# Two-block transformer kernel: product order behind three norms, place of the splits, a wait for GpSimd's masks

## The reference

```python
def rms_norm_2(x, gain):
    xf = x.astype(jnp.float32)
    y = xf * lax.rsqrt(jnp.mean(xf * xf, axis=-1, keepdims=True) + NORM_EPS)
    return (y * gain.astype(jnp.float32)).astype(x.dtype)

def swiglu_2(h, w_gate, w_up, w_down):
    return (jax.nn.silu(h @ w_gate) * (h @ w_up)) @ w_down
```

## Time and profile before

| | |
|---|---|
| executions shown | 1966.95, 1968.44, 1965.23 us; median 1966.95 |
| the profiled execution | 1967.34 us; span of its instructions 1965.5 us |
| mean granted clock of TensorE | 0.975 of full |
| PE busy | 1848.6 us, 94% of the span, 15010 matmuls |
| DVE busy | 1156.8 us, 59% |
| ACT busy | 770.1 us, 39% |
| POOL busy | 300.6 us, 15% |
| DMA | 266 MB, mean 135 GB/s |
| chain that ended last | PE 75%, DVE 12%, POOL 5%, ACT 5%, rest 3% |

### The profile page before, as it was taken

How to read it: one execution, slowest core, us unless ns; L and a number is a source line. 1 busy time by engine, 2 the same in 40 slices (tenths; PEclk the granted TensorE clock), 3 DMA queues, 4 the chain that set the end, 5 groups by cost and what they waited for, 6 DMA issues and landing times.

```text
span 1965.5 us, 34448 instructions
## 1 busy us (share of the span) xinstructions
PE 1848.6 (94%) x15010; PEld 1629.9 (83%) x15010; DVE 1156.8 (59%) x1715; ACT 770.1 (39%) x1073; POOL 300.6 (15%) x264
## 2 busy tenths in 40 slices
PE   7999888999999978987999999999998999999998
PEld 5777556878888868856999999989988778899997
DVE  4643575554353337666655486555767778576654
ACT  4432563221122224455443443343455444344332
POOL 0011001899180010100000100002001111000000
PEclk9998998999999988999999999999999999999999
DMA  8344212565353222203555655544431111245551
GB/s 347 107 156 177 75 44 86 175 212 189 135 182 125 87 76 70 81 22 108 174 191 174 214 182 179 186 150 158 153 119 45 45 45 67 88 172 177 188 187 71
DMA packets 40759, 266.24 MB, mean 135 GB/s; under 512 B 4512, under 2 KB 4640, under 8 KB 13344
## 3 DMA queue, kind: packets, MB, share of 16 engines
q1 hardware_dynamic: 35712, 244.10, 35.5%
q0 software_dynamic: 4608, 16.78, 2.7%
q10 hardware_dynamic: 288, 3.15, 0.4%
HBM read 262.96 MB, written 1.05 MB: 134 GB/s over the span
## 4 chain that ended last, share of the span: by engine, by line
PE 75%; DVE 12%; POOL 5%; ACT 5%; issue 2%; DMA 2%; DVEq 0%; ACTq 0%; POOLq 0%
PE ps L641 18%; PE ps L643 18%; PE ps L642 18%; DVE W L621 2%; POOL work L1101 2%; PE ps L1641 2%; POOL work L1102 1%; PE ps L1003 1%; PE ps L647 1%; PE ps L1428 1%; PE ps L648 1%; PE ps L649 1%; PE ps L2372 1%; ACT W L612 1%; PE ps L2390 1%
## 5 line engine op out<-in xcount | busy, mean ns | idle before, releaser
L621 DVE TENSOR_TENSOR W<-ring,W 128x2048 fp32r<-128x2048 f32 (+2 forms) x194 | 439.5, 2267 | 247.2 <-ACT W L612 246.8
L612 ACT ACTIVATE W<-ring 128x2048 fp32r<-128x2048 f32 (+2 forms) x194 | 359.2, 1854 | 123.9 <-PE ps L643 114.0
L641 PE MATMUL ps<-h_lat,W 128*128 128x256 f32 x1056 | 301.4, 285 | 6.1 <-DVE h_lat L807 4.2
L643 PE MATMUL ps<-h_lat,W 128*128 128x256 f32 x1056 | 299.4, 283 | 0.0
L642 PE MATMUL ps<-h_lat,W 128*128 128x256 f32 x1056 | 299.4, 283 | 0.0
L641 PEld LDWEIGHTS ps<-h_lat,W 128*128 128x128 f32 x1056 | 203.2, 192 | 8.2 <-issue 4.6
L642 PEld LDWEIGHTS ps<-h_lat,W 128*128 128x128 f32 x1056 | 203.3, 193 | 0.3 <-issue 0.2
L643 PEld LDWEIGHTS ps<-h_lat,W 128*128 128x128 f32 x1056 | 203.3, 192 | 0.0
L748 POOL TENSOR_TENSOR work<-work 128x256 f32<-128x256 f32 (+1 forms) x42 | 41.1, 977 | 955.7 <-ACT work L730 768.5
L984 DVE TENSOR_TENSOR work<-work,ps 128x256 f32<-128x256 f32 (+1 forms) x88 | 43.0, 488 | 189.2 <-ACT work L959 189.1
L641 PE MATMUL ps<-hidden_lat,W 128*128 128x256 f32 x528 | 149.4, 283 | 0.0
(11 more groups left out here) (405 smaller groups left out, 4308.6 us busy)
## 6 DMA issues: line engine op xcount, KB each, us to landing
ring<-w_up_dram SPq DMA_DIRECT2D x88, 1024.0 KB, 4.9
ring<-w_down_dram SPq DMA_DIRECT2D x43, 1024.0 KB, 4.9
ring<-w_ada_dram SPq DMA_DIRECT2D x32, 1024.0 KB, 6.5
work<-w_ada_dram POOLq DMA_DIRECT2D x32, 512.0 KB, 4.1
ring<-w_rkv_dram SPq DMA_DIRECT2D x13, 1024.0 KB, 4.9
ring<-w_fm_dram SPq DMA_DIRECT2D x10, 1024.0 KB, 5.0
ring<-w_out_dram SPq DMA_DIRECT2D x8, 1024.0 KB, 4.9
ring<-w_gates_dram SPq DMA_DIRECT2D x16, 512.0 KB, 3.6
```

What stands on the lines that cost most here:

```text
L612: act.activation(slots[SLOT[s]][:, 0, 0:cols], ring[:, u % RING, 0:cols], ACT.Copy).then_inc(w_high, 1)
L621: dve.tensor_tensor(slots[SLOT[s]][:, 1, 0:cols], ring[:, u % RING, 0:cols], slots[SLOT[s]][:, 0, 0:cols], ALU.subtract).then_inc(w_low, 1)
L641: pe.matmul(o, slots[SLOT[s]][:, 0, at:at + cols], high, start=first, stop=False)
L643: return pe.matmul(o, slots[SLOT[s]][:, 1, at:at + cols], high, start=False, stop=final)
```

## The change

Four edits.

1. In `dve_residual` and `act_residual`, where a norm follows, the split of the last step (m = 7) is no longer made ahead of that step, but behind all 8 steps, with the same argument.
2. In `act_high` for norm 0, ACT makes the split of the second unit of tma0 behind the first tile's high parts; ahead of it stays the first unit's.
3. Behind norms 1, 3 and 6 PE takes each arriving tile for two results. At norm 1 these are the gate and the up half of the first unit (two banks of PSUM), at norm 3 the gate halves of the first two units of up1, at norm 6 the first feature tiles of the first two units of qk. The other halves follow. The number of matmuls stays.
4. In `pool_rwkv` GpSimd waits, ahead of the second of its five masks, for `rw_T0`, DVE's end of L2713.

```diff
@@ dve_residual
             for m in range(KT):
-                dve_split(dve, s0 + ((m + 1) * kt - 1) // TPU + 1 + AHEAD)
+                if m < KT - 1 or norm is None:
+                    dve_split(dve, s0 + ((m + 1) * kt - 1) // TPU + 1 + AHEAD)
...
             if norm in LATE:
                 dve_late_low(dve, norm, KT - 1)
+            if norm is not None:
+                dve_split(dve, s0 + (KT * kt - 1) // TPU + 1 + AHEAD)
@@ act_residual
             for m in range(KT):
-                act_split(act, s0 + ((m + 1) * kt - 1) // TPU + 1 + AHEAD)
+                if m < KT - 1 or norm is None:
+                    act_split(act, s0 + ((m + 1) * kt - 1) // TPU + 1 + AHEAD)
...
+            if norm is not None:
+                act_split(act, s0 + (KT * kt - 1) // TPU + 1 + AHEAD)
@@ act_high
                     ins.then_inc(h_high, 1)
+                if r == 0 and m == 0:
+                    act_split(act, FIRST_OF_KIND["tma0"] + 2)
@@ pe_ffn
                 for i in range(f):
                     s, g = FIRST_OF_KIND[up] + i, FIRST_GROUP[up] + i
-                    bank = pe_group(pe, g)
+                    bank = GROUPS[g][0] if r == 1 and i == 1 else pe_group(pe, g)
                     pe_weights(pe, s)
+                    if r == 0 and x == 0 and i == 0:
+                        for k in range(KT):
+                            pe_h_tile(pe, norm, k)
+                            for half in range(2):
+                                mm = weight_tile(pe, ps[:, bank + half, 0:n], s, (half * KT + k) * P, P, h[:, k, 0, :], h[:, k, 1, :],
+                                                 k == 0, k == KT - 1)
+                        mm.then_inc(group_done, 1)
+                        continue
+                    if r == 1 and i == 0:
+                        pe_weights(pe, s + 1)
+                        second = pe_group(pe, g + 1)
+                        for k in range(KT):
+                            pe_h_tile(pe, norm, k)
+                            for y, b in ((0, bank), (1, second)):
+                                weight_tile(pe, ps[:, b, 0:n], s + y, k * P, P, h[:, k, 0, :], h[:, k, 1, :], k == 0, k == KT - 1)
                     for half in range(2):
+                        if r == 1 and i < 2 and half == 0:
+                            continue
@@ pe_qkv (two_tiles loses its arguments norm and late)
+            for i in range(2):
+                banks.append(pe_group(pe, g0 + i))
+                pe_weights(pe, s0 + i)
+            for k in range(KT):
+                pe_h_tile(pe, 6, k)
+                for i in range(2):
+                    weight_tile(pe, ps[:, banks[i], 0:T], s0 + i, k * P, P, h_mix[:, k, 0, :], h_mix[:, k, 1, :], k == 0, k == KT - 1)
+            for i in range(2):
+                for k in range(KT):
+                    mm = weight_tile(pe, ps[:, banks[i], T:2 * T], s0 + i, (KT + k) * P, P, h_mix[:, k, 0, :], h_mix[:, k, 1, :],
+                                     k == 0, k == KT - 1)
+                mm.then_inc(group_done, 1)
             for i in range(6):
-                two_tiles(pe, "qk", i, h_mix[:, :, 0], h_mix[:, :, 1], 6 if i == 0 else None)
+                if i >= 2:
+                    two_tiles(pe, "qk", i, h_mix[:, :, 0], h_mix[:, :, 1])
@@ pool_rwkv
                 for l in range(1, LEVELS):
+                    if l == 2:
+
+                        pool.wait_ge(rw_T0, g + 1)
@@ scalar engine's program
                 if layer:
                     act_root(act, 2 * layer)
-                act_split(act, FIRST_OF_KIND[f"tma{layer}"] + 2)
+                    act_split(act, FIRST_OF_KIND[f"tma{layer}"] + 2)
+                else:
+                    act_split(act, FIRST_OF_KIND["tma0"] + 1)
```

More of the change, by code:

```diff
@@ L913, in pe_ffn @@
                     s, g = FIRST_OF_KIND[up] + i, FIRST_GROUP[up] + i
-                    bank = pe_group(pe, g)
+                    bank = GROUPS[g][0] if r == 1 and i == 1 else pe_group(pe, g)
                     pe_weights(pe, s)
+                    if r == 0 and x == 0 and i == 0:
[13 more added lines that the diff above has]
+                                weight_tile(pe, ps[:, b, 0:n], s + y, k * P, P, h[:, k, 0, :], h[:, k, 1, :], k == 0, k == KT - 1)
                     for half in range(2):
+                        if r == 1 and i < 2 and half == 0:
+                            continue
                         o = ps[:, bank + half, 0:n] if n == TA else ps[:, bank, half * n:(half + 1) * n]
                         for k in range(KT):
-                            if x == 0 and i == 0 and half == 0:
+                            if r != 1 and x == 0 and i == 0 and half == 0:
                                 pe_h_tile(pe, norm, k)
@@ L1934, in build, with two_tiles @@
         wa2, g2a, g2b = (a(D) for _ in range(3))
-        def two_tiles(pe, phase, i, high, low, norm=None, late=None):
+        def two_tiles(pe, phase, i, high, low):
             s, g = FIRST_OF_KIND[phase] + i, FIRST_GROUP[phase] + i
@@ L1944, in two_tiles @@
                 for k in range(KT):
[L1945 to L1948, removed]
                     mm = weight_tile(pe, ps[:, bank, m * T:(m + 1) * T], s, (m * KT + k) * P, P, high[:, k, :], low[:, k, :],
@@ L1956, in pe_qkv @@
         def pe_qkv(pe):
+            s0, g0 = FIRST_OF_KIND["qk"], FIRST_GROUP["qk"]
+            banks = []
+            for i in range(2):
[10 more added lines that the diff above has]
+                mm.then_inc(group_done, 1)
             for i in range(6):
-                two_tiles(pe, "qk", i, h_mix[:, :, 0], h_mix[:, :, 1], 6 if i == 0 else None)
+                if i >= 2:
+                    two_tiles(pe, "qk", i, h_mix[:, :, 0], h_mix[:, :, 1])
                 if i == 2:
```

## The result

Four executions of the changed kernel took 1948.26 to 1954.33 us, median **1952.8**; four of the kernel before, in the same comparison, 1965.23 to 1968.44, median 1967.64. The ratio is 0.9931, with an interval of 0.9911 to 0.9952: 0.7% faster. The profiled execution is the fastest of the four, 1948.26 (span 1946.4), mean clock 0.982 against 0.975.

A forecast was written before the change was run, and what follows sets the result against it. PE was the bound, busy 94% of the span. Terms -7.0 - 1.3 - 2.7 + 2.9 - 1.2 - 0.6 = -9.9 us took the profiled 1967.34 to 1957.4, median 1957.0, range 1952.5 to 1962.

The forecast's parts named there:

- rival A: Whole kernel: 1951 to 1954 us, as norm 1's 3 us come through or both low-clock stretches vanish; chance 0.13.
- GpSimd's masks, 7.0 us: Recurrence, four groups: holding back four masks shortens L2712 and L2713 to 0.69 and wins 7.0 us, bounds 0 to 7.5.
- Low clock behind the waits, 1.3 us: Recurrence: one of two low-clock stretches behind PE's waits vanishes, winning 1.3 us, bounds 0 and 2.6.
- Norm 2, 2.7 us: Norm 2 (down0_1): residual starts sooner with VectorE's split moved behind it; reciprocal 2.7 us earlier, bounds 2.0 to 3.2.
- Norm 6's split, +2.9 us: Norm 6 (down2): moved splits hold ACT's root and then the reciprocal; 2.9 us lost, bounds 1.1 and 3.0.
- Norm 4 and norm 0, 0: Norm 4 (down1) and norm 0: later splits cost 0, with 1.6 us cover at norm 4, at most 0.1 at norm 0.
- Norm 1, 0 us with bounds of 1: Norm 1 (up0_0): PE wins about 3 us but then waits for GpSimd's sums; 0, bounds 1 lost to 1 won.
- Norm 3, 1.2 us with bounds of 0.6 and 1.8: Norm 3 (up1): two results per tile keep PE busy while rows arrive, winning 1.2 us, bounds 0.6 and 1.8.
- Norm 6's order, 0.6 us: Norm 6 (qk): two results per tile win 0.6 us, PE being nearly full already; bounds 0 and 1.2.
- Rival C: Norms 3 and 6: alternating two PSUM banks keeps the clock low through all 96 products; 1975.6 us, chance 0.03.

The follow-up runs named there:

- third comparison: Side by side against the kernel before: the changed kernel, 1947.65 us, ratio 0.9907, and it with the split moved at norm 2 alone, 1950.13 us, 0.9918.
- wait_first: The kernel before, with GpSimd's wait ahead of all five masks: 1955.85 us, ratio 0.9958.
- pool_only: The kernel before with GpSimd's wait ahead of its second mask alone: 1957.25 us, ratio 0.9952.
- norm2_late: The changed kernel with splits moved at norm 2 alone, VectorE's left to the place behind the third scaled tile: 1953.18 us, ratio 0.9933 to the kernel before.
- start_only: The kernel before with only ACT's second-unit split of tma0 at norm 0 moved behind the first tile: 1965.51 us, ratio 1.0004.
- order_only: The kernel before with the two results per tile behind norms 1, 3 and 6 alone: 1963.31 us, ratio 0.9988.
- split_norm2: The changed kernel with the residual split moved at norm 2 alone: 1950.75 us, ratio 0.9922 to the kernel before; again 1950.13 us, 0.9918.

## Why the prediction was right or wrong

The median came 4.2 us below the 1957.0 predicted and at the edge of its range, 1952.5 to 1962; it lies in rival A's span of 1951 to 1954, and one of A's two conditions, both low stretches gone, was met. That the median lies inside the range is in part luck: it depends on how many of the executions ran at which clock (see the end of this section), and in the third comparison the same kernel took 1947.65, below the range.

- **GpSimd's masks, 7.0 us: right.** L2711 stayed at 1.23, L2712 and L2713 came to 0.68, the waits went from 7.5 to 0.3 us. wait_first shows the cause: an instruction of VectorE with two operands in SBUF that meets one of GpSimd's is held until that ends (the reduction beside the masks, 0.68, is not). The Trainium skill (SBUF — State Buffer, the section Who interferes with whom) says the same, an exclusive lock for the whole instruction and not a share of a rate. These runs agree.
- **Low clock behind the waits, 1.3 us: mis-sized.** I took one of two low stretches to vanish. Both did, in every kernel that has edit 4 and in wait_first, and each had cost 1.5 to 1.6 us, not 1.3: 3.1 us, above the bound of 2.6. The price was too low by the factor 0.8, the busy share of the whole window: the idle part of it, PE's wait, lay ahead of the low stretch, and within the stretch PE was busy for all of its 3.4 us. The four groups together gave 10.5 us (1.14 + 3.57 + 3.61 + 2.21) for a predicted 8.3.
- **Norm 2, 2.7 us: right in the pair**, 2.94, with the split in front of the reciprocal, as worked out. I had counted 0.84 of it for a faster sum of squares; that part is the clock's, and pool_only has it without the edit. Against it 2.06 are left, near the lower bound of 2.0. norm2_late prices that split at 0.30 (0.5 taken), and nothing in the end.
- **Norm 6's split, +2.9 us: right**, +2.74 in all kernels that move it, by the mechanism given: first ACT's root, then the reciprocal stands behind a split. That taking it back won nothing in the medians of the comparison side by side I had not expected; at a like clock it may have (see there).
- **Norm 4 and norm 0, 0: right.** 4 to 6 differs by norm 6's amount alone, start_only is 1.0004.
- **Norm 1, 0 us with bounds of 1: wrong**, -1.35 in the changed kernel, -1.2 in order_only. The step that failed is that GpSimd's sums leave at the same time. PE reached its first sums 3.1 us sooner against the reciprocal (30.22 us behind it, 33.34 before) and waits four times, as foreseen. But GpSimd came sooner too. VectorE's split and GpSimd's product of the second unit that meet, the unit's last addition and PE's second call, before and after:

```profile
365.51 2.28 DVE L621 TENSOR_TENSOR W<-ring,W 128x2048 fp32r<-128x2048 f32 x1
365.74 3.82 POOL L1101 TENSOR_TENSOR work<-work,const 128x1024 f32<-128x1024 f32 x1 [0.26 <-DMA work<-w_ada_dram]
...
371.82 0.73 POOL L1105 TENSOR_TENSOR work<-work 128x256 f32<-128x256 f32 x1
...
373.87 0.50 PE L1115 MATMUL ps<-const,work 128*128 128x1 f32 x4
```

```profile
357.69 2.82 DVE L621 TENSOR_TENSOR W<-ring,W 128x2048 fp32r<-128x2048 f32 x1
...
359.28 3.01 POOL L1126 TENSOR_TENSOR work<-work,const 128x1024 f32<-128x1024 f32 x1
...
364.54 0.72 POOL L1130 TENSOR_TENSOR work<-work 128x256 f32<-128x256 f32 x1
...
365.41 0.58 PE L1140 MATMUL ps<-const,work 128*128 128x1 f32 x4 [0.71 <-POOL work L1130]
```

  The product, 1.92 us alone, met nearly the whole of a split before and only the rest of one after: 3.82 against 3.01. The second unit's sums end 42.39 us behind the reciprocal instead of 43.40, the third's 54.7 instead of 55.9, and every later one some 1.3 sooner. I had named this as the bound (splits that hit the sums in other places) and put it at 1 us.
- **Norm 3, 1.2 us with bounds of 0.6 and 1.8: not one number**, 0.3 in the profiled pair, outside the bounds, and 1.6 in the other two runs of the changed kernel, inside them. The sum was made for one length of the low stretch, and that is not a constant of the kernel. **Norm 6's order, 0.6 us**: 0.2 in the profiled pair, 0.95 in the other two, likewise.
- **Rival C** did not happen: the alternation between two banks ran at the upper clock once the low stretch was over. The Trainium skill (TensorE: Matmul & The Clock Gate, the section on a second failure mode) tells of a kernel whose clock went up and down while it cycled through PSUM banks. No window behind norms 1, 3 and 6 shows that: there the clock rose once and stayed up.

Together the steps now give -10.5 - 2.9 - 1.35 + 2.7 - 0.2 - 0.3 = -12.6 us for the profiled pair, of its 19.1. The rest is **the stretch ahead of norm 1**, -6.0, and small changes in 0 and 2 to 3. It is a stretch at the low clock in the mLSTM, 13.7 us long, that the kernel before has at 149.5 us and the changed one has not. The same window of before, after and wait_first:

```profile
149.00:163.00 14.00, 14.00 (x66) 12.14 (x66) 3.16 (x8) 0.39 (x1) 0.00 (x0) 0.52 0.45 171
```

```profile
149.00:163.00 14.00, 14.00 (x105) 10.84 (x104) 6.68 (x18) 1.86 (x5) 0.87 (x2) 1.00 0.58 204
```

```profile
149.00:163.00 14.00, 14.00 (x105) 10.82 (x104) 6.67 (x18) 1.86 (x5) 0.87 (x2) 1.00 0.55 201
```

66 matmuls against 105 in 14 us. wait_first has the code of before in all of this part and still runs like after; split_norm2, whose code there is that of after, has the low stretch, in both of its runs. pool_only and order_only, with the code of before, have none at 149 and one of 10.2 us at 274 instead. In stretch 0 to 1 the four kernels at 294.6 to 295.4 us have 13.7 us at the low level, the nine at 297.2 to 303.6 have 23.9 to 30.7. So no edit made here decides it, and what does is open.

It is no constant of the changed kernel either. The unprofiled executions show no stretches, but each one's mean granted clock is on record. Of the 15 executions of the changed kernel eight ran at 0.980 to 0.982 and took 1945.8 to 1950.1 us, median 1947.6, all three profiled ones among them; the other seven ran at 0.976 to 0.979 and took 1952.7 to 1954.6, median 1953.2. The kernel before took 1961.6 at 0.980 and 0.981 (8 of the 51 in the three later comparisons) and 1965.2 at 0.976 to 0.979 (21). At a like clock the gain is thus 14.0 or 12.0 us. That is close to what the steps give: 12.6 for the first pair, and some 2 more where norms 3 and 6 give 1.6 and 0.95. The three gains in the medians, 14.8, 13.8 and 18.2 us, mix the two: one, two and five of the executions of the changed kernel ran at 0.980 or more.

## What to carry to other kernels

If VectorE and GpSimd both work out of SBUF ahead of a product, let the one that nobody waits for begin its long series only when the critical one is through, but let it make the first piece, which the product needs too. Move work from ahead of a short chain (residual, square, sum, root, reciprocal) only where it really makes that chain start late: where PE is late itself, as at norm 6, the work lands inside the chain. And when two kernels are compared within 1%, cut both at instructions that they share and look at the clock in each piece: two effects of one edit here cancelled within 0.2 us in the total, and the second largest difference of the profiled pair, 6.0 us, belonged to no edit. Set beside one another only executions of about the same granted clock: the same kernel took 1947.6 or 1953.2 us by it.

## What was not expected of the hardware

- A low stretch can come where the records show PE busy all the time: in the window at 149 us above PE is busy 14.00 of 14 us in all three kernels, and in the 4 us ahead of it (145 to 149) it is busy 4.00 us with 23 matmuls in before and in after alike. Busy is not full here: twelve of the 23 have 2 columns each. But the same matmuls were followed by the low level in the one and not in the other.
- A low stretch vanished at two places once the wait in front of it fell from 2.15 us to none (in wait_first to 0.86), and its cost (1.5 to 1.6 us each) was three quarters of the wait itself. Behind group 3's wait, as long as theirs, there was none.
- The lock works both ways: while GpSimd's sums run beside VectorE's splits, an addition of 0.73 us takes up to 2.67, and a split of 2.28 takes up to 4.51. The three masks behind GpSimd's first took 1.7 each beside VectorE's instructions and 1.27 alone.
